# First layer: early part on other banks and slots, and residual gates copied to all partitions by DMA

## The reference, cut to what matters

```
m_lat = jnp.split((silu_c @ mod_w[layer] + mod_b[layer])[:, None, :], 6, axis=-1)
h_lat = rms_norm(x_lat, norm1_g[layer]) * (1 + m_lat[1]) + m_lat[0]
...                      # y_lat, y_ctx = even_mixer(...) or odd_mixer(...)
x_lat = x_lat + m_lat[2] * y_lat
h_lat = rms_norm(x_lat, norm2_g[layer]) * (1 + m_lat[4]) + m_lat[3]
x_lat = x_lat + m_lat[5] * expert_choice_ffn(h_lat, router_w[layer], ...)
```

## Time and profile before

| | |
|---|---|
| median of 3 runs | 2378.73 us |
| the profiled execution | 2380.57 us |
| its span, first to last instruction | 2378.8 us |
| mean granted TensorE clock | 0.939 of full speed |
| busy: PE, DVE, ACT, POOL | 2016.2, 1002.1, 749.0, 7.1 us |
| read from HBM | 640.30 MB, 270 GB/s over the span |
| chain that ended last: PE, DMA, DVE, ACT | 61%, 32%, 3%, 2% |

### The profile page before, as it was taken

How to read it: one execution, slowest core, us unless ns; L and a number is a source line. 1 busy time by engine, 2 the same in 40 slices (tenths; PEclk the granted TensorE clock), 3 DMA queues, 4 the chain that set the end, 5 groups by cost and what they waited for, 6 DMA issues and landing times.

```text
span 2378.8 us, 37875 instructions
## 1 busy us (share of the span) xinstructions
PE 2016.2 (85%) x16424; PEld 1502.7 (63%) x16424; DVE 1002.1 (42%) x1908; ACT 749.0 (31%) x1338; POOL 7.1 (0%) x16
## 2 busy tenths in 40 slices
PE   4889988979797889766565655999999999998998
PEld 3767764535353566644343443888888878887887
DVE  2255441313131544501010103665666766556776
ACT  3145320000000435300000002656455446554544
POOL 0000000000000000000000000000000000000000
PEclk8999989999999999887787887999999999999999
DMA  8846449999999712299999998333555543345451
GB/s 348 319 178 260 201 197 428 427 426 428 427 427 427 294 71 107 108 427 427 426 426 426 426 426 329 142 142 142 181 195 191 181 173 142 139 167 199 177 192 74
DMA packets 45571, 643.78 MB, mean 271 GB/s; under 512 B 5168, under 2 KB 5440, under 8 KB 6496
## 3 DMA queue, kind: packets, MB, share of 16 engines
q1 hardware_dynamic: 44352, 637.14, 66.4%
q0 software_dynamic: 1056, 4.23, 0.5%
HBM read 640.30 MB, written 1.05 MB: 270 GB/s over the span
## 4 chain that ended last, share of the span: by engine, by line
PE 61%; DMA 32%; DVE 3%; ACT 2%; issue 1%; SPq 0%; DVEq 0%; ACTq 0%; POOLq 0%
PE bank L881 58%; DMA ring<-in_stream 31%; PE bank L889 3%; DMA arena<-in_b_masks 0%; DVE weights_low L2439 0%; DVE tokens_low L2004 0%; ACT arena L1831 0%; ACT ring L1706 0%; DVE arena L2539 0%; DVE ring L2242 0%; ACT arena L1589 0%; ACT weights_high L1543 0%; ACT arena L1575 0%; DVE x L2055 0%; DVE arena L2169 0%
## 5 line engine op out<-in xcount | busy, mean ns | idle before, releaser
L881 PE MATMUL bank<-ring,arena 128*32 128x128 f32 (+4 forms) x7928 | 637.9, 381 | 226.4 <-DMA ring<-in_stream 222.0
L881 PEld LDWEIGHTS bank<-ring,arena 128*32 128x32 f32 (+1 forms) x7928 | 376.4, 135 | 458.8 <-DMA ring<-in_stream 282.9
L2439 DVE TENSOR_TENSOR weights_low<-ring,weights_high 128x1024 fp32r<-128x1024 f32 (+2 forms) x288 | 343.4, 1194 | 274.2 <-ACT weights_high L1543 269.1
L1543 ACT ACTIVATE weights_high<-ring 128x1024 fp32r<-128x1024 f32 (+2 forms) x288 | 297.8, 1035 | 285.5 <-PE bank L881 284.9
L881 PE MATMUL bank<-weights_high,tokens_high_low 128*128 128x512 f32 (+2 forms) x1152 | 359.3, 386 | 12.0 <-DVE tokens_high_low L2451 10.0
L881 PEld LDWEIGHTS bank<-weights_high,tokens_high_low 128*128 128x128 f32 x1152 | 215.4, 190 | 57.2 <-DVE tokens_high_low L2451 10.6
L1543 ACT ACTIVATE arena<-bank 128x256 f32<-128x256 f32 (+6 forms) x254 | 104.4, 435 | 396.3 <-PE bank L889 306.9
L881 PE MATMUL bank<-weights_low,tokens_high_low 128*128 128x512 f32 (+2 forms) x576 | 219.2, 381 | 0.0
L2159 DVE TENSOR_TENSOR arena<-arena,bank 128x256 f32<-128x256 f32 (+1 forms) x64 | 22.7, 354 | 457.3 <-PE bank L881 457.3
L1667 ACT ACTIVATE arena<-bank 128x256 f32<-128x256 f32 (+1 forms) x64 | 21.1, 330 | 588.9 <-PE bank L881 588.9
L2169 DVE TENSOR_TENSOR arena<-bank,arena 32x512 f32<-32x512 f32 (+1 forms) x128 | 70.9, 554 | 265.3 <-PE bank L881 264.0
(11 more groups left out here) (206 smaller groups left out, 2111.9 us busy)
## 6 DMA issues: line engine op xcount, KB each, us to landing
ring<-in_stream SPq DMA_DIRECT2D x302, 2048.0 KB, 22.0
x<-in_x_in SPq DMA_DIRECT2D x1, 2048.0 KB, 10.5
arena<-in_od_pack POOLq DMA_DIRECT2D x1, 1024.0 KB, 12.7
arena<-in_gains POOLq DMA_DIRECT2D x2, 512.0 KB, 5.8
out<-arena SPq DMA_DIRECT2D x1, 1024.0 KB, 4.0
arena<-in_b_masks POOLq DMA_DIRECT2D x1, 896.0 KB, 11.2
arena<-in_ev_pack POOLq DMA_DIRECT2D x1, 582.0 KB, 9.1
ring<-in_ev_pack POOLq DMA_DIRECT2D x1, 512.0 KB, 11.6
```

The lines of the kernel that those rows point to most:

```text
L881: ins = pe.matmul(o, lhsT, rhs, start=start, stop=stop)
L1543: ins = act.activation(o, i, ACT.Copy)
L2439: dve.tensor_tensor(dst, whole, high.bitcast(F32), ALU.subtract).then_inc(sig, 1)
```

## The change

What it does, part by part:

- The four early modulation chunks and the first `mod_cols` all go to bank 7, one after the other. The norm's transposes then have banks 0 to 7 in this order. PE does 28 of the 32 transposes ahead of the fourth chunk, and the four of k = 7 last.
- Later modulation chunks use slot 4 twice besides slots 2 and 3. In the table `EV_MODS`, chunks 8 to 11 of the first layer move from steps 8, 9, 10 and 12 to steps 9, 11, 13 and 14, and the first two of the second layer from steps 17 and 18 to 18 and 19. What saves their results moves from step 14 to 15.
- The first POOL load, `in_ev_pack` to a ring slot, waits for the fourth chunk in place of the second.
- `mod_row` is gone on PE and ACT. POOL's `spread_gates` does its work in two stages: four DMAs gather two rows of 1024 numbers on partition 0 of `bc` (each takes 4 pieces of 128 numbers from 4 partitions); when these have landed, two DMAs copy each row from partition 0 to the other 127. It is called three times: when the attention output has been cut in halves, after the last residual addition of the mixer, and after the last expert's gated output.
- DVE waits for the copies ahead of the first residual addition (32), after the first one-hot tiles (64), and both ACT and DVE ahead of `norm_split("n1_1", ...)` (96).

```diff
@@ -95,13 +95,13 @@
-EV_MODS = {**dict(zip((1, 3, 5, 7, 8, 9, 10, 12), ((0, c) for c in range(4, 12)))),
-           **dict(zip((17, 18, 20, 21, 22, 23, 24, 26, 27, 28, 30, 31), ((1, c) for c in range(12))))}
-MODS_SAVED = 14
+EV_MODS = {**dict(zip((1, 3, 5, 7, 9, 11, 13, 14), ((0, c) for c in range(4, 12)))),
+           **dict(zip((18, 19, 20, 21, 22, 23, 24, 26, 27, 28, 30, 31), ((1, c) for c in range(12))))}
+MODS_SAVED = 15
 SGU_STATS, SGU_ROOT, SGU_V, SGU_AT = (24, 25), 26, 27, 31
 CAT_HEADS = {26: 0, 27: 1, 29: 2, 31: 3}
 CAT_TURNS = {34: (4, 5), 35: (6, 7)}
-GATE_ROWS = {36: 0, 37: 1, 38: 2, 39: 3}
@@ -239,11 +239,11 @@
-ALL_BANKS, GEMM_BANKS, ATT_BANKS = range(BANKS), range(0, 4), range(4, 8)
+ALL_BANKS, GEMM_BANKS, ATT_BANKS, LAST_BANK = range(BANKS), range(0, 4), range(4, 8), range(7, 8)
 def _tickets():
     turns = [0] * BANKS
-    at = {ALL_BANKS: 0, GEMM_BANKS: 0, ATT_BANKS: 0}
+    at = {ALL_BANKS: 0, GEMM_BANKS: 0, ATT_BANKS: 0, LAST_BANK: 0}
@@ -259,10 +259,8 @@
-            stage("mod0", range(MOD_EARLY))
-            stage("modcol0", [0])
-        else:
-            stage("modrow1", 4)
+            stage("mod0", range(MOD_EARLY), LAST_BANK)
+            stage("modcol0", [0], LAST_BANK)
@@ -283,8 +281,7 @@
-                if p in GATE_ROWS:
-                    stage("modrow0", [GATE_ROWS[p]], ATT_BANKS)
@@ -303,8 +300,6 @@
-        if layer == 0:
-            stage("modrow5", 4)
@@ -344,7 +339,9 @@
-EVZ_SLOTS, MOD_SLOTS = (0, 1), (2, 3)
+EVZ_SLOTS = (0, 1)
+EARLY_SLOTS = (4, 5, 2, 3)
+MOD_SLOTS = (4, 2, 3, 4, 2, 3, 2, 3) + (2, 3) * 6
@@ -358,12 +355,12 @@
-        put(("mod0", c), (SPARE_SLOTS + MOD_SLOTS)[c])
+        put(("mod0", c), EARLY_SLOTS[c])
     for n in range(2):
         put(("evz", EVZ_ORDER[n]), EVZ_SLOTS[n])
     mods = [(f"mod{layer}", c) for layer, c in EV_MODS.values()]
     for n, key in enumerate(mods):
-        put(key, MOD_SLOTS[n % 2])
+        put(key, MOD_SLOTS[n])
@@ -399,7 +396,7 @@
-    return LOADS_OF[n] - 1 + (SLOT_OF[n] in SPARE_SLOTS and LOADS_OF[n] > 1)
+    return LOADS_OF[n] - 1 + (SLOT_OF[n] in SPARE_SLOTS and n >= CHUNK_AT["moe0", 0])
@@ -847,7 +844,7 @@
-            Banks(pool).filled("mod0", 1)
+            Banks(pool).filled("mod0", MOD_EARLY - 1)
@@ -856,6 +853,27 @@
+            spreads = [0]
+
+            def spread_gates(rows):
+
+                for half, (src, s) in enumerate(rows):
+                    for c in range(2):
+                        load(bc[0:1, half, c * 512:(c + 1) * 512].rearrange("p (q j) -> p q j", q=4), src[s:P:32, c * P:(c + 1) * P], "gate_row")
+                spreads[0] += 1
+                pool.wait_ge(sem("gate_row"), 64 * spreads[0])
+                for half in range(2):
+                    load(bc[1:P, half, :], bc[0:1, half, :].unsqueeze(1).to_broadcast([1, P - 1, D]), "gates")
+
+            pool.wait_ge(sem("cat_lo"), EV_PAIRS)
+            spread_gates([(mrow2, s) for s in range(2)])
+
+            pool.wait_ge(sem("x_mix"), 8)
+            spread_gates([(mrow5, s) for s in range(2)])
+
+            Banks(pool).drained("moe0", (GROUPS - 1, PER_GROUP - 1, "y"))
+            spread_gates([(mrow[:, 2 * v * P:(2 * v + 2) * P], 0) for v in (2, 5)])
@@ -903,11 +921,11 @@
-            def norm(name, xn, tiles, ready, count):
+            def norm(name, xn, tiles, ready, count, ks=range(KD)):
                 for t in range(tiles):
                     pe.wait_ge(ready, count - tiles + t + 1)
-                    for k in range(KD):
+                    for k in ks:
@@ -969,13 +987,6 @@
-            def mod_row(name, n, src, s):
-
-                b.vacant(name, n)
-                for qq in range(2):
-                    at = 32 * (2 * (n % 2) + qq) + s
-                    mm(bank(name, n)[:, qq * 256:(qq + 1) * 256], ident[:, at:at + 1].to_broadcast([P, P]), src, True, True,
-                       fills(name, n) if qq == 1 else None)
@@ -1027,10 +1038,6 @@
-                if layer == 0:
-
-                    for n in range(4):
-                        mod_row("modrow5", n, mrow5, n // 2)
@@ -1141,12 +1148,14 @@
-            for c in range(MOD_EARLY):
+            for c in range(MOD_EARLY - 1):
                 mod_chunk(0, c)
             pe.wait_ge(sem("base_in"), 16)
+            norm("n1_0", xn4, 4, sem("xn"), 4, range(KD - 1))
+            mod_chunk(0, MOD_EARLY - 1)
             b.drained("mod0", MOD_EARLY - 1)
             mod_cols(0, 0)
-            norm("n1_0", xn4, 4, sem("xn"), 4)
+            norm("n1_0", xn4, 4, sem("xn"), 4, [KD - 1])
@@ -1224,9 +1233,6 @@
-                if p in GATE_ROWS:
-                    pe.wait_ge(sem("mod_saved"), 1)
-                    mod_row("modrow0", GATE_ROWS[p], mrow2, GATE_ROWS[p] // 2)
@@ -1235,9 +1241,6 @@
-            for n in range(4):
-                v = 2 + 3 * (n // 2)
-                mod_row("modrow1", n, mrow[:, 2 * v * P:(2 * v + 2) * P], 0)
@@ -1653,10 +1651,6 @@
-                if layer == 0:
-                    act.wait_ge(sem("x_mix"), 8)
-                    for n in range(4):
-                        mod_row("modrow5", n)
@@ -1747,9 +1738,8 @@
-            for n in range(4):
-                mod_row("modrow1", n)
             b.drained("modcol1", 1)
+            act.wait_ge(sem("gates"), 96)
@@ -2181,6 +2171,8 @@
+                if layer == 0:
+                    dve.wait_ge(sem("gates"), 64)
@@ -2315,8 +2307,7 @@
-                        for n in range(4):
-                            b.drained("modrow0", n)
+                        dve.wait_ge(sem("gates"), 32)
@@ -2331,6 +2322,7 @@
+            dve.wait_ge(sem("gates"), 96)
```

More of the change, by code:

```diff
@@ L1617, in z_split @@
                 copy(high, src, sem("z_w_hi"))
-            def mod_row(name, n):
-                b.filled(name, n)
-                dst = bc[:, n // 2, :].rearrange("p (c q j) -> p q c j", c=2, q=4)[:, 2 * (n % 2):2 * (n % 2) + 2]
-                copy(dst, bank(name, n)[:, :].rearrange("p (q c j) -> p q c j", q=2, c=2), frees(name, n))
             def cat_split(width):
@@ L1734, in after_slot @@
                     copy(z_hi[:, k, :], bank("cat0", k)[:, :], sem("cat_hi"))
-                if p in GATE_ROWS:
-                    act.wait_ge(sem("cat_lo"), EV_PAIRS)
-                    mod_row("modrow0", GATE_ROWS[p])
             for p in range(A_END):
```

## The result

| | before | changed |
|---|---|---|
| median of 4 runs | 2379.39 us | 2427.33 us |
| runs | 2377.65 to 2381.08 | 2425.80 to 2429.92 |
| span of the profiled execution | 2378.8 us | 2425.3 us |

The changed kernel is slower: ratio 1.0203, 95% interval 1.0185 to 1.022, against 2428 forecast.

The account below looks back on a forecast made before the run. The weight-chunk ring was taken to bound the first layer's experts, with PE carrying the path ahead. Terms -5.8 - 12.0 - 1.9 - 3.7 + 16.5 + 22 + 34.3 = +49.4 gave 2428 us, range 2360 to 2455.

Parts of the forecast that it names:

- The price of a spread: POOL's gate copies: 50.0 us each, 39.0 of it data from one source partition; 13.4 at the lower end.
- Mixer gates and first spread: Mixer steps 36 to 39: gate matmuls leave PE, -3.7; DVE's wait at the first residual addition starves PE, +16.5.
- Second: Second spread, from the last residual addition: delays the scaling of gathered tokens and so the first expert chunk, +22.
- Third: Third spread, from the last expert's gated output: delays the second layer's norm, +34.3.
- The early part: Everything ahead of the spreads: start -5.8, slot 4 and chunk steps -12.0, moved last chunk -1.9.
- The start: Transposes ahead of the fourth chunk: ACT begins 2.3 earlier, PE's first projection at 44.7 for 50.47, -5.8.
- The slots and the moved chunk: Modulation loads: both ring waits and their slow clock go, -12.0; last chunk moves from step 12 to 14, -1.9.
- My sign: Check on PE's early stretch: the forecast is wrong if step 16 doesn't begin 18 to 21 us earlier.
- fast: Rival at the three spreads: 16 engines run without sharing a source port, -16.3, 2362 us; chance 0.17.
- half price: Rival at the three spreads: two rows read side by side, 19.5 us, -5.9, 2373 us; chance 0.06.
- the early gain stays: Opposite rival: hand-offs or ring take the gain back; 2438 with slow spreads (within 0.73), 2373 with fast (0.04).
- The ring does suffer: Rival: one engine carries all rows, third spread some 12 us longer, first some 6, 2446; counted within the 0.73.

Follow-up runs that it names:

- h_all: Changed kernel with each gate row gathered into HBM and read back from there for all 128 partitions; 2360.25 us, ratio 0.9923.
- t_all: Changed kernel with two-level copies within SBUF, partition 0 to 31 others, then those 32 to the other 96; 2367.12 us, ratio 0.995.
- two_src: Changed kernel with the gate row gathered into partitions 0 and 64, each feeding the 63 behind it; 2397.52 us, ratio 1.0083.
- h_127: `h_all` with each large copy writing partitions 1 to 127 and a 4 KB copy writing the first; 2367.69 us, ratio 0.9957.
- m_all: Changed kernel with all three gate fills by matmuls as before, keeping its early part; 2353.36 us, ratio 0.9904.
- d_first: `m_all` with only the first fill (mixer gates) by the two-stage DMA; 2368.59 us, ratio 0.9965.
- d_second: `m_all` with only the second fill (expert gates of the first layer) by DMA; 2378.15 us, ratio 1.0007.
- d_third: `m_all` with only the third fill (second layer's gates) by DMA; 2387.53 us, ratio 1.0045.
- h_two_m: `h_all` with the third fill by matmuls as in the kernel before; 2350.77 us, ratio 0.9889.
- s_old: `m_all` with the old ring slots and modulation chunk steps, keeping only the new start; 2370.91 us, ratio 0.997.
- b_old: `m_all` with the old start, keeping only the new ring slots and modulation chunk steps; 2361.25 us, ratio 0.9928.
- h_pre: `h_all` with the second and third spreads' small copies issued right behind the first spread; 2355.35 us, ratio 0.9909.

## Why the prediction was right

*The price of a spread*, the step on which all hung, was forecast at 50.0 us and came out at 50.0 (220.46 to 270.49). Its parts were off in both directions: the small copies land 6.5 to 7.1 after the last issue (6.3 forecast), the large ones take 39.2 to 40.2 where 2.7 and 39.0 were added up. The reason given, one source partition, is shown: the source was moved (`h_all`), multiplied by 32 (`t_all`) and by two (`two_src`), and each made the copies faster, while the number of rows did nothing of the kind (`h_127`). My way to the number was not the mechanism: I took the share of one of 16 engines, 26.7 GB/s, and the trace shows all 16 occupied. What limits is the source side. That the share of one engine and the rate of one source partition are nearly the same number is luck. Whether the limit belongs to a single partition or to some group of neighbours, no run separates.

The Trainium skill's rule, "SBUF — State Buffer", section "Door 1: The DMA port swizzle", puts the limit at the port of the partitions and measured 27.6 GB/s; this case's 26 to 27 GB/s from partition 0 agree. The same section puts partitions 0 and 64 on different ports. Twice the rate was my own conclusion from that, and `two_src` gave 1.5 times. What that skill's "DMA: Bandwidth & Descriptors" says in the section on why a DMA increments its semaphore by 16, that 127 partitions may fall on one engine, did not happen in either form here: in the changed kernel all engines are busy, and in `h_127` 508 KB land in 11.1 us. I had left out that the section itself names an exception for some copies that GpSimd issues on trn2, with 127 partitions on all 16 engines; the trace agrees with that.

I also took the load of 512 KB in 3.9 us for one whose source is many partitions. Its source is HBM, and the partitions were on its receiving side. By the Trainium skill's fit ("DMA: Bandwidth & Descriptors", section "Anatomy of one DMA"), which I had said it agrees with, it would take an estimated 3.2 us.

*Mixer gates and first spread*: -3.7 and +16.5 forecast, together +12.8. From the fourth high/low pair to the last addition the trace has +13.8 (25.1 less 11.3). The matmuls that are gone are worth 4.8 and not 3.7 (`h_all` against `m_all`, 29.9 for 34.7 us), so the spread itself costs +18.6. `d_first`, against fills by matmuls, is +15.2.

*Second*: +22 forecast, +22.3 in the trace (486.79 us from last addition to last expert output before, 509.10 after). `d_second` +24.8, since it is measured against `m_all`, where the second fill's matmuls and the 64 behind them run faster than before. Part of it is not the wait: the 96 matmuls behind it take 13.27 instead of 10.58.

*Third*: +34.3 forecast, +34.2 in the trace and in `d_third`. ACT's wait there is 40.38 and not 34: before, ACT copied the gate rows and waited for PE in the same stretch. DVE's waits at the other two are 20.73 and 27.57, as forecast.

*The early part* was the step that was mis-sized: -19.7 forecast, with bounds around it, -25.1 in the trace. One trace is good to some 2 us here: in the kernels with the same early part the fourth pair begins at 218.3 (`m_all`) to 221.9 (`h_two_m`). Three terms of it:
- The start: -5.8 forecast, -8.5 measured. 1.2 of that is an earlier first landing of the ring (PE's first chunk at 17.47, before 18.64), which is no effect of the change: `d_first` and `t_all` have the same start, with 17.82 and 19.27. Of the other 7.3, 4.0 are ACT's earlier beginning (37.37, before 42.51), where I had 2.3, and 3.3 the way from there to PE's first projection, where I had 3.5. ACT gained more because the fourth chunk ran in 1.95 instead of 3.64, at a granted clock of 1.00 instead of 0.50. I had kept PE's slow clock at this place; with 28 transposes right ahead of it the chunk is fast. It began 0.8 late where I had 0.4. PE still waits 3.89 there, for DVE's first low half, so that the 7.3 look like ACT's old wait of 7.29 only by accident.
- The slots and the moved chunk: -13.9 forecast, -13.0 measured at step 16. "No ring wait over 1 us up to 110" was wrong: one of 1.17 has come at step 1 and one of 1.79 is left at step 14. I had said the steps between release and use are enough for every load.
- Behind step 16 a further -3.6 that I had counted as nothing. PE begins that step at a granted clock of 1.00, before at 0.50 (0.50 us for the first matmul, before 0.77), and all that follows moves with it. My sign was a step 16 that is 18 to 21 earlier; 21.45 lies just outside, and 20.3 without the earlier landing inside.

*The second fill's 16 matmuls*: I said that leaving them out gains 1.4, which the wait hides. With the early start it costs 3.5, as `m_all` and `h_two_m` show (28.95 and 32.46 us from the last addition to the first expert matmul; 7.41 and 9.71 for the 64). The wait hid that too.

The halves run alone agree with these sizes: `s_old` -7.1 for the start (7.3), `b_old` -16.8 for the slots (13.0 and 3.6).

*The rivals.* The spread is neither fast nor half price, and the early gain stays. The ring does suffer, though no single engine carries the rows: from 745 to 810 us, with the third spread in it, its chunks land 34.9 us after their issue in `d_third` (median), and 16.4 in `m_all`. But the spread doesn't last longer for it (39.7 in the chain, the other two 40.2 and 39.2), which is what that rival asked for. My range's own bounds were added up wrong: 2428 less 11 and 5 is 2412 and not 2408, and 2428 and 18 and 10 is 2456.

So the norm of the second layer came +45.2 instead of +49.4: 5.4 more gained by the early part, 1.0 more lost at the first spread with its matmuls. The rest of the program added 1.3, to the 46.5 of the end; where, no run shows. The medians lie 47.9 apart. That the forecast of 2428 was met within 1 us is therefore luck. What is shown is the shape, and the price of a spread.

## What to carry to other kernels

A broadcast out of one SBUF partition costs what that one partition gives, however many DMA engines pull: count the bytes written, divide by 26 GB/s (measured from partition 0), and compare with the time until the first reader; if it must be a transfer, go through HBM or by levels, and gather ahead of the wait. Matmuls that fill a gap of PE may pay for themselves where what follows them then runs at the higher clock, as the 64 in `m_all` do (7.41 us, without them 9.71); in `d_first` the same 16 brought less (9.0). When a change has a part that gains and a part that loses, run each alone before judging it: here 24 us of gain were hidden under 74 of loss, and the better kernel was the half of the change.

## What the runs showed of the hardware that was not expected

- A copy whose rows all come from one partition keeps all 16 DMA engines at a share of 0.9 while 26 GB/s move. What else is queued then is slowed: `in_od_pack`, 1 MB behind the third spread in the same queue, landed in 41.3 us, and in 10.3 to 17.6 in `t_all`, `m_all`, `h_pre` and `h_all`. The ring's loads come from SP's queue and are slowed too: from 808 to 848 us, beside the third spread, all transfers together move 145 GB/s at a share of 0.97, after 427 in the experts' stretch.
- Two source partitions, 0 and 64, gave 40 GB/s, not 52.
- Four small copies of 2 KB, four rows each, take 6.5 to 7.1 us in the chain, whether into SBUF (the changed kernel) or HBM (`h_all`, 6.9); the eight of `two_src` 4.6 to 9.5.
- 254 KB from one partition take 11.97 us, and the 786 KB behind them from 32 partitions 8.37.

Left open: a version with the first row through HBM and the other two fills by matmuls, which the clock rows speak for (an estimate from the 3.5 us above: some 3 us under `h_two_m`), was not run, nor one whose two sources take turns within a copy.
